# Moving the split activations to other byte distances from the split weights

## What is computed

```python
h = rmsnorm(x, g_mix) * (1 + scale1) + shift1
proj = h @ w_in                                   # q, k, v, gates
merged = sigmoid(ga) * (oa @ w_branch_dil) + sigmoid(gb) * (ob @ w_branch_na)
x = x + gate1 * (merged @ w_out)
u = depthwise_conv_seq(h2 @ w_up, conv_w, conv_b)
x = x + gate2 * ((gelu(u_gate) * u_val) @ w_down)
```

## Time and profile before

| | us |
|---|---|
| median of 3 runs | 1755.56 (1752.27 to 1755.82) |
| profiled execution, its own time | 1753.67 |
| its span, first to last instruction | 1751.9 |
| PE busy | 1683.1 (96%) |
| DVE busy | 1265.3 (72%) |
| ACT busy | 868.2 (50%) |
| mean granted TensorE clock | 0.998 |

### The profile page before, as it was taken

One profiled execution on the slowest core, in us unless ns is written; L12 is line 12 of the kernel. 1 busy time (PEld: TensorE's weight loads), 2 busy tenths in 40 slices (PEclk: granted clock), 3 DMA queues, 4 the chain that ended last, 5 costly groups with the idle time before them and its releaser, 6 DMA issues.

```text
span 1751.9 us, 29656 instructions
## 1 busy us (share of the span) xinstructions
PE 1683.1 (96%) x12356; PEld 1559.9 (89%) x12356; DVE 1265.3 (72%) x1835; ACT 868.2 (50%) x1219; POOL 21.8 (1%) x39
## 2 busy tenths in 40 slices
PE   2999999998999999999999999999999999999998
PEld 2999889987999889988989998999889989989996
DVE  6777879978787666676768775777666666768653
ACT  4555465553533364666463444544365665474332
POOL 0000000000000000000000000000000000000000
PEclk9999999999999999999999999999999999999999
DMA  9878646558587954755647786677744745537452
GB/s 384 311 255 240 252 165 219 219 203 349 187 287 285 288 184 171 200 181 207 227 141 280 281 232 257 216 289 280 289 166 169 215 180 202 209 146 273 180 181 110
DMA packets 70934, 398.93 MB, mean 228 GB/s; under 512 B 8208, under 2 KB 8464, under 8 KB 36112
## 3 DMA queue, kind: packets, MB, share of 16 engines
q1 hardware_dynamic: 67392, 386.06, 62.3%
q0 software_dynamic: 2976, 9.47, 1.6%
q10 hardware_dynamic: 432, 1.50, 0.2%
HBM read 395.92 MB, written 1.08 MB: 227 GB/s over the span
## 4 chain that ended last, share of the span: by engine, by line
PE 81%; DVE 5%; DVEq 4%; ACT 3%; DMA 3%; issue 2%; ACTq 1%; SPq 1%
PE lin L420 17%; PE lin L421 17%; PE lin L422 17%; PE att L555 17%; DVEq L1486 3%; PE att L654 3%; DMA ada_w<-in_ada 2%; PE lin L458 2%; PE lin L460 2%; PE lin L468 1%; PE pt L681 1%; DVEq L1482 1%; DVE work L1483 1%; PE att L704 1%; DMA raw<-in_w 1%
## 5 line engine op out<-in xcount | busy, mean ns | idle before, releaser
L1159 DVE TENSOR_TENSOR lo<-raw,hi 128x2048 fp32r<-128x2048 f32 x262 | 599.7, 2290 | 282.6 <-ACT hi L803 282.4
L420 PE MATMUL lin<-h_hi,hi 128*128 128x256 f32 x2480 | 700.9, 283 | 6.8 <-DVE work L1483 6.8
L421 PE MATMUL lin<-h_lo,hi 128*128 128x256 f32 x2480 | 692.7, 279 | 0.0
L422 PE MATMUL lin<-h_hi,lo 128*128 128x256 f32 x2480 | 691.4, 279 | 0.0
L803 ACT ACTIVATE hi<-raw 128x2048 fp32r<-128x2048 f32 x262 | 500.8, 1912 | 215.0 <-PE att L555 125.1
L420 PEld LDWEIGHTS lin<-h_hi,hi 128*128 128x128 f32 x2480 | 466.1, 188 | 10.1 <-issue 9.8
L421 PEld LDWEIGHTS lin<-h_lo,hi 128*128 128x128 f32 x2480 | 466.3, 188 | 1.1 <-issue 1.0
L422 PEld LDWEIGHTS lin<-h_hi,lo 128*128 128x128 f32 x2480 | 466.1, 188 | 0.0
L1175 DVE CUSTOM_DVE_ANT_0 ada_w<-ada_w,cs 128x1024 f32<-128x1024 f32 x179 | 217.8, 1218 | 24.4 <-DMA ada_w<-in_ada 24.2
L1019 ACT ACTIVATE work<-lin 128x256 f32<-128x256 f32 x88 | 33.8, 384 | 282.3 <-PE lin L422 273.9
L555 PE MATMUL att<-hi,act_hi 128*128 128x512 f32 x440 | 136.6, 392 | 3.7 <-DVE lo L1159 3.7
(11 more groups left out here) (253 smaller groups left out, 2017.5 us busy)
## 6 DMA issues: line engine op xcount, KB each, us to landing
raw<-in_w SPq DMA_DIRECT2D x269, 1024.0 KB, 4.8
ada_w<-in_ada SPq DMA_DIRECT2D x179, 512.0 KB, 5.4
ada_s<-in_ada SPq DMA_DIRECT2D x13, 512.0 KB, 16.5
bias<-in_bias POOLq DMA_DIRECT2D x16, 256.0 KB, 4.7
ffn_row<-rows POOLq DMA_DIRECT2D x5, 512.0 KB, 9.4
x<-in_x ACTq DMA_DIRECT2D x1, 1024.0 KB, 6.9
dcon<-in_dcon SPq DMA_DIRECT2D x1, 1024.0 KB, 7.5
ra<-rows POOLq DMA_DIRECT2D x2, 512.0 KB, 5.2
```

What stands on the lines that cost most here:

```text
L420: mm(out, w_hi, a_hi, start=start, stop=False, skip_group_check=skip)
L421: mm(out, w_hi, a_lo, start=False, stop=False, skip_group_check=skip)
L422: return mm(out, w_lo, a_hi, start=False, stop=stop, skip_group_check=skip)
L1159: tt(lo[c % SPLIT][:], raw[:, c % RAW, :], hi[c % SPLIT][:].bitcast(F32), ALU.subtract).then_inc(*s_lo.up(c))
```

## The change

The order, number and kind of all instructions stay. The shift tensors change, and the high and low part of h, of act and of br get shifts of their own. `br_shift` in front of `ra` goes away. `obr_shift` stays, but what lies in front of it has grown by 288 bytes.

```diff
         x = sb("x", [P, 2, D])
-        sb("h_shift", [P, 72])
+        sb("h_hi_shift", [P, 64])
         h_hi = sb("h_hi", [P, KT, SEQ], F32R)
+        sb("h_lo_shift", [P, 80])
         h_lo = sb("h_lo", [P, KT, SEQ], F32R)
...
         with ExitStack() as scope:
+            sb("act_hi_shift", [P, 120], F32, scope)
             act_hi = sb("act_hi", [P, FT, SEQ], F32R, scope)
+            sb("act_lo_shift", [P, 80], F32, scope)
             act_lo = sb("act_lo", [P, FT, SEQ], F32R, scope)
...
         with ExitStack() as scope:
-            sb("br_shift", [P, BR_SHIFT], F32, scope)
             ra = sb("ra", [P, 15, SEQ], F32, scope)
             rb = sb("rb", [P, 12, SEQ], F32, scope)
+            sb("br_hi_shift", [P, 64], F32, scope)
             br_hi = sb("br_hi", [P, 12, SEQ], F32R, scope)
+            sb("br_lo_shift", [P, 24], F32, scope)
             br_lo = sb("br_lo", [P, 12, SEQ], F32R, scope)
```

## The result

The changed kernel takes 1778.07 us (median of 4 runs, 1777.16 to 1779.80), the kernel before on the same chip 1754.26 us. The ratio is 1.0141, with a 95% interval from 1.0129 to 1.0154: it is slower by 1.4%. The forecast was 1749, the range 1725 to 1771; the result lies above the range, and the kernel moved the other way than forecast.

A forecast was written before the change was run, and what follows sets the result against it. The prediction took PE's step from one matmul to the next as the bound. Its terms, -10.1+7.0-0.3-1.6-0.7 = -5.7 us, took the profiled 1753.67 us to 1748.0; it forecast 1749, range 1725 to 1771.

The forecast's parts named there:

- the rival in which the addresses do nothing: Whole kernel: moving addresses changes no matmul step, by the skill's two independent read ports; 1753.7 us, chance 0.10.
- term (1): 8160 matmuls with h moving: two thirds go to distance 256, unchanged; one third to 64, at the floor; -10.1 us.
- the passing assumption: PE's moving read passes the next tile's load once modulo 512 bytes, costing 3.3 to 6.4 ns unless level or slightly ahead.
- the hi pairs get dearer: h-moving pairs going to 256 rise by 2.8 ns, +15.2 us; 1763 us; chance 0.36 shared with the empty 64 pairs.
- deciding point of 118.1: Step in ns of the h-moving pairs that go to 256, above which the kernel was to be slower.
- the gain of the 64 pairs: One third of h-moving matmuls (2720) go to distance 64 and fall to the floor, -3.7 ns each, -10.1 us.
- the empty 64 pairs: h-moving pairs at 64 bring nothing: +4.4 us remains, 1758; chance 0.36 shared with the hi pairs get dearer.
- Term (2): 1320 down matmuls leave distance 0: 880 go to 256, +5.6 us, 440 to 64, +1.4; sum +7.0, bounds 0 and +8.4.
- (5): 576 v-projection matmuls, h stationary, go from 288 to 256 and 64: no change, bounds -2.7 to +1.2 us.
- (6): Attention's full-fp32 matmuls get other distances as everything behind h moves: 0, bounds 2 us to either side.
- term (3): 288 out matmuls: hi goes to 256 at the same price, lo (96) to 64 at half of it; -0.3 us.
- Term (4): Branches: br hi goes to 32, floor, -1.6 us; br lo to 128, nothing; obr to 64, floor, -0.7 us.

The follow-up runs named there:

- the bare sweep: Separate kernel of matmuls alone, other engines idle, 32 distances from stationary to moving tile: 113.3 to 120.0 ns for 256 columns, 226.7 to 234.7 for 512.
- `h_hi_only`: Kernel before with h_hi alone moved to distance 256, h_lo left at 288: 1771.80 us against 1755.15, ratio 1.0093.
- `act_only`: Kernel before with act_hi and act_lo alone moved, to 256 and 64: 1760.91 us against 1755.26, ratio 1.0029.
- `all_112`: Kernel before with both halves of h, br and obr at distance 112 (or 368), act at 256: 1731.23 us against 1753.66, ratio 0.9871.

## Why the prediction was wrong

What bounds the kernel was read rightly: PE's steps changed, and its waits stayed within 0.2 us in all. The addresses were added up rightly. The floor of 113.4 ns, got as half of 226.9, was met by the runs at 113.3. That the address matters, against the Trainium skill (SBUF — State Buffer, "Who interferes with whom": two independent read ports), stands: in the bare sweep the same matmul takes from 113.3 to 120.0 ns. That is what the chip shows here, and the rival in which the addresses do nothing falls with it.

The step that failed is term (1), through the passing assumption under it. It had two parts. "Two thirds go from 288 to 256: no change" measured 120.0 ns, +2.9. "One third goes to 64: the floor" measured 117.6 alone and 121.5 in the stream of 0.up0, where 113.4 was taken; that 120.0 is the mean of the three steps there. Together the form gained +17.4 us instead of losing 10.1, and this difference of 27.5 us is nearly all of the 29 between forecast and result. Beneath it the assumption was wrong in its period (256 bytes, so 288 is 32, and 256 is 0), in its shape (a small lead isn't quiet for 256 columns), and in adding thirds, since the mix locks into one rhythm. The rows of before held only two distances for each form. 0.out was not one of 288: from its stationary h to the moving weights it is 224, the other sign. "256 lies between 224 and 288, and 288 costs less" was an interpolation across a curve that jumps by 6 ns within 16 bytes.

The rival "the hi pairs get dearer" had the right sign and the right half of h (`h_hi_only`), and its price of 119.9 ns meets the measured mean of 120.0; its deciding point of 118.1 was passed. That the price fits is in part luck: it was carried over from 0.out by the passing assumption, and in the stream it is not the hi pairs alone that pay. It came out at 1763 because it kept the gain of the 64 pairs, while the empty 64 pairs were told as a case apart. Both failed at once: -5.7+15.2+10.1 = +19.6 gives 1773, and with the branches, which paid 0.8 us instead of gaining 2.3, 1776. The range was too narrow for that reason: two terms that rest on one assumption were varied one at a time.

Term (2) was right in size: down steps at 231.1 ns, where the working gives 226.9 and 7.0 us/1320 = 5.3, so 232.2, and +5.7 us by `act_only` for +7.0. Its reason was not: act_hi at 256 costs nothing for 512 columns, and act_lo at 64, beside it, does. In the trace of after it is 4.4 us, in that of `act_only` 6.7. The steps are the same in both; the rest lies in the down stage of the first block, where PE waits for chunks. In `act_only`, as in before, one of these waits is long enough that the granted clock stands at the 1.2 GHz level for 3.4 us behind it; in after they are shorter there and the clock stays up. First `act_only`, then after:

```profile
396.55 0.94 PE L557 MATMUL att<-hi,act_hi 128*128 128x512 f32 x2 [2.65 <-DVE lo L1161]
396.90:400.30 3.40, 3.40 (x10) 0.50 1.03 416
```
```profile
396.21 0.73 PE L559 MATMUL att<-hi,act_hi 128*128 128x512 f32 x2 [0.92 <-DVE lo L1163]
394.00:399.00 5.00, 4.08 (x18) 1.00 1.02 419
```

Terms (5) and (6) measured -0.2 and +1.9 us, within their bounds; term (3), without bounds, -0.6 for -0.3. Term (4) fell with the passing assumption: branches at 117.6, not 114.5. The last claim, that nothing else becomes the bound at 3% more speed, held in `all_112`, at the price of 4.4 us more of waiting.

## What to carry to other kernels

Where a stream of matmuls is the bound, the addresses of stationary and moving tiles are a parameter like any other, here worth from +1.4% to -1.3% with not an instruction changed. It can't be interpolated: measure the curve with a bare kernel of matmuls, in steps of 16 bytes, counted from the stationary to the moving tile, for each shape and with the real order of operands, and repeat each point after different work, because the same distance can have a quiet and a dear rhythm. And when two terms of a sum rest on one assumption, let them fail together in the range.

## What the runs showed of the hardware that was not expected

The step of fp32r matmuls depends on the distance between the tiles modulo 256 bytes, and it does so with all other engines idle: with one distance throughout, 113.3 to 120.0 ns for 256 columns and 226.7 to 234.7 for 512. The least step was 113.3 at every width of the stationary tile. The Trainium skill (TensorE: Matmul & The Clock Gate, "Back-to-back issue gap") gives 262 cycles between isolated matmuls of 256 columns, that is an estimate of 109 ns at 2.4 GHz; no run here settled there. The stream falls into steady rhythms of its own, kept over 960 matmuls, and at a distance of 192 bytes the same 48 matmuls settled at 113.3 or at 117.8 ns, by what ran before them. Which of PE's reads meet, what in the work before chooses the rhythm, and why a narrower load moves the dear distances instead of thinning them evenly, stays open.
